# Third layer's input projections: rows turned by token halves, other PSUM banks, pool products moved into the attention

## The chip, the cores and the metric

The kernel is one program on one core of one Trainium2 chip. The metric is the device time in microseconds. Three runs of the kernel before took 1465.88, 1466.32 and 1468.25 us, median 1466.32. Engines: TensorE (PE in the profile, its weight loads PEld), VectorE (DVE), ScalarE (ACT), GpSimd (POOL) and SyncE (SP), which issues the loads of the weights. Each engine works through its own list of instructions in order, and waits on semaphores that the others raise.

## The reference, cut to what matters

256 tokens of width 1024 pass two transformer layers and then a third one, whose start is the place of this case. `ctx` is a second set of 256 tokens, `mod` a vector worked out from a condition, which shifts and scales the normalized rows.

```python
hx = modulate(rmsnorm(x, norm1_g[l]), sh1, sc1)          # the 256 tokens
hc = modulate(rmsnorm(ctx, norm1_g[l]), sh1c, sc1c)      # the 256 context tokens
qx, kx, vx, px = split_projection(hx @ w_in[l])          # 512, 128, 128 and 512 columns
qx = apply_axial_rope(qx, rope)
kx = apply_axial_rope(kx, rope)
kc, vc = split_kv(hc @ w_in[l][:, ATTN_WIDTH:ATTN_WIDTH + 2 * KV_WIDTH])
attn_x = latent_window_attention(qx, kx, vx, kc, vc, attn_sink[l])   # 8 heads, keys of x and of ctx
pool_x = multiscale_pool(px, pool_w[l], pool_scale[l])   # 4 groups: window mean minus token, then 128x128, then scale
x = x + g1 * (jnp.concatenate([attn_x, pool_x], axis=-1) @ w_out[l])
# then: rmsnorm, modulate, a router and 64 experts of which each token takes 8, and a last rmsnorm
```

All is float32.

## The kernel before

Tokens lie in two tiles of 128 rows (token halves 0 and 1). For a product TensorE needs the features on the partitions, so normalized rows are turned by TensorE: 8 transposes a half (`turn_rows`, recorded at L628) write two PSUM banks, and then ACT takes the first four tiles of the half and DVE the other four, multiplying by the scale and adding the shift on the way (`take_turn_mod`, L1350 and L1673). `xT` holds the columns of the tokens, `cT` those of the context. For the turn named `rms1`, half 0 goes through banks 4 and 5 and half 1 through 6 and 7.

Weights stream through a ring of 8 slots of 1 MB; SP issues the load of a slot once TensorE has raised `chunks_used` for what was in it. The third layer's input weights `in_2` are five chunks: keys and values (1), queries (2), pooled columns (2).

The stretch on TensorE runs so. After the last product of the second layer's MLP (L833) it waits for DVE's last addition (`mlp_added`), makes two broadcast rows of the modulation (`mod_row`, L756; banks 2 and 3, then 0 and 1; ACT copies each into `gaterow`), then the context's keys (bank 2, L1051) and values (bank 3, L1055), then turns both halves of x (`rows_ready` comes from DVE, which normalizes half 0 and then half 1), waits for all columns, and makes the keys and values of x. The query panel (L656, banks 0 and 1) follows, the rotation of the keys for the rope (L670, bank 4), then a wait for the finished rope (`roped`), as the pooled panel (L661) writes bank 4 again. The rotation of the queries (banks 6 and 7) follows that panel, then the pool products (L1081: the pooled columns times a matrix that holds the window means; ACT copies the result, `dT`), a small product for the second modulation (L749, bank 0), and the products with the pool weights (L1089, banks 6 and 7), which ACT scales into `xT` (L1592). Only then does the attention start.

The attention (`attention`) goes through 16 units (8 heads for each half of the tokens; numbers 80 to 95 of the program). Each turn of its loop handles several units at once: at even i the scores of units i and i+1 (L701), the turn of the probabilities of unit i-3 (L720), the product with the values of unit i-4 (L732). DVE masks the scores and takes the row maximum (L1806), ACT takes the exponential (L1372), DVE copies the turned probabilities out of PSUM (L1816). Scores of these units lie in banks 0, 1, 6 and 7, turned probabilities in 2 and 3, the results of the first eight units in one of banks 4 and 5 and those of the other eight in the other. `attention` takes `pieces`, other work of TensorE to be placed into given turns of the loop; without any it runs `keep_warm`, two matmuls of 512 columns whose result is not read (L620), after each of the first two pairs of scores. ACT and DVE have `hooks` in their own loops for the same purpose.

The order is written out by hand, engine by engine; no scheduler moves anything. TensorE's third layer stands from L1042 on, ACT's from L1565, DVE's from L2090.

## Time and profile before

| | |
|---|---|
| median of three runs | 1466.32 us |
| the profiled execution | 1468.9 us |
| its span, first to last instruction | 1467.2 us |
| TensorE busy | 1426.4 us (97%) |
| DVE busy | 457.5 us (31%) |
| ACT busy | 210.9 us (14%) |
| POOL busy | 67.5 us (5%) |
| DMA, mean over the span | 251 GB/s |
| mean granted TensorE clock | 0.993 |

The span is that of one execution under the profiler; the profiled execution's own time is 1.7 us longer. A busy share of 97% for TensorE says that it rarely waits, not that it works at its peak. Float32 matmuls appear as two records each, transposes as one, so counts in the timeline are counts of records. Rows of a timeline give start, duration and what was done; a bracket at the end gives the idle time before and who ended it. In the rows of the chain of waits, the durations are cut so that they add up to the span. In the rows by window, the busy time of each engine is followed by the granted clock (1.00 is 2.4 GHz, 0.50 is 1.2 GHz), the DMA engines' busy share and their GB/s.

### The profile page before, as it was taken

Reading aid. Unit: us, or ns where it says so; the run is one execution under the profiler, and the core shown is the slowest. Engines: PE = TensorE matmul, PEld = TensorE weight load, DVE = VectorE, ACT = ScalarE, POOL = GpSimd, SP = SyncE. Lnnn points to the kernel's source line nnn. Section 1 sums busy time; section 2 is a strip of 40 time slices with the busy share of each in tenths; the row PEclk is TensorE's granted clock in tenths of the full one; section 3 lists DMA queues with packets and bytes.
Section 4 is the critical chain, followed back from the end, with each engine's and each line's share of the span. In section 5 each row is a group of like instructions: output and inputs, shape, how many; then the busy total and the mean of one; then the engine's idle time right before and its main releaser. Section 6 shows DMA issues by size and latency. Waiting matters only on the chain.

```text
span 1467.2 us, 17841 instructions
## 1 busy us (share of the span) xinstructions
PE 1426.4 (97%) x6990; PEld 887.1 (60%) x6990; DVE 457.5 (31%) x1035; ACT 210.9 (14%) x515; POOL 67.5 (5%) x101
## 2 busy tenths in 40 slices
PE   8999999999999999999999999999999999999985
PEld 7676585675658867577575675744454445444542
DVE  1136442422542355242245063422111111111113
ACT  2135200000002331000012141200000000000001
POOL 1016200000000010000000000000000000000000
PEclk9999999999999999999999999999999999999997
DMA  9721174464264335664634405589999999998993
GB/s 394 293 82 59 58 275 184 143 245 184 86 229 145 115 116 213 248 254 183 243 148 158 152 21 207 206 346 378 421 421 404 422 421 421 418 421 331 422 421 157
DMA packets 51833, 368.45 MB, mean 251 GB/s; under 512 B 5856, under 2 KB 6064, under 8 KB 7984
## 3 DMA queue, kind: packets, MB, share of 16 engines
q1 hardware_dynamic: 46080, 333.57, 57.0%
q0 software_dynamic: 5392, 32.05, 6.0%
q10 hardware_dynamic: 288, 1.80, 0.3%
q8 instruction: 52, 0.85, 0.2%
q14 instruction: 21, 0.17, 0.0%
HBM read 366.32 MB, written 1.05 MB: 250 GB/s over the span
## 4 chain that ended last, share of the span: by engine, by line
PE 86%; DVE 3%; DMA 1%; issue 0%; ACT 0%; SPq 0%; DVEq 0%
PE ps L833 15%; PE ps L815 13%; PE ps L1222 13%; PE ps L1172 7%; PE ps L1246 6%; PE ps L1204 6%; PE ps L771 6%; PE ps L656 5%; PE ps L732 2%; PE ps L661 2%; PE ps L701 2%; DMA vec_rows<-in_stream 1%; PE ps L794 1%; PE ps L1015 1%; PE ps L1122 1%; PE ps L628 1%
## 5 line engine op out<-in xcount | busy, mean ns | idle before, releaser
L833 PE MATMUL ps<-ring,qk_tiles 128*128 128x512 f32 x512 | 221.4, 592 | 0.0
L815 PE MATMUL ps<-xT,ring 128*128 128x256 f32 x896 | 194.7, 379 | 0.0
L815 PEld LDWEIGHTS ps<-xT,ring 128*128 128x128 f32 x896 | 170.1, 190 | 25.6 <-issue 2.9
L833 PEld LDWEIGHTS ps<-ring,qk_tiles 128*128 128x128 f32 x512 | 97.1, 190 | 118.1 <-issue 117.7
L1222 PE MATMUL ps<-ring,masked_and_probs 128*32 128x512 f32 (+2 forms) x488 | 150.9, 603 | 0.4 <-DMA par<-in_stream 0.4
L1172 PEld LDWEIGHTS ps<-masked_and_probs,mix_rows 128*128 128x128 f32 x896 | 102.5, 192 | 20.8 <-issue 20.8
L656 PE MATMUL ps<-xT,ring 128*128 128x256 f32 x496 | 110.6, 385 | 0.8 <-DVE xT L1666 0.8
L1172 PE MATMUL ps<-masked_and_probs,mix_rows 128*128 128x128 f32 x896 | 107.0, 278 | 0.0
L656 PEld LDWEIGHTS ps<-xT,ring 128*128 128x128 f32 x496 | 95.4, 193 | 14.5 <-issue 1.2
L1204 PE MATMUL ps<-masked_and_probs,probT 128*128 128x512 f32 x216 | 97.2, 593 | 1.0 <-DVE masked_and_probs L2213 1.0
L1246 PE MATMUL ps<-ring,probT 128*32 128x512 f32 (+2 forms) x264 | 83.7, 597 | 1.6 <-DVE probT L2208 1.6
L771 PE MATMUL ps<-ring,xT 128*128 128x512 f32 x192 | 84.0, 593 | 0.0
L1355 ACT ACTIVATE masked_and_probs<-ps 128x512 f32<-128x512 f32 (+1 forms) x62 | 36.5, 593 | 319.4 <-PE ps L1246 185.2
L1222 PEld LDWEIGHTS ps<-ring,masked_and_probs 128*32 128x32 f32 (+2 forms) x488 | 44.3, 128 | 55.6 <-issue 55.5
L1222 PE MATMUL ps<-qk_tiles,masked_and_probs 128*32 128x512 f32 (+2 forms) x248 | 74.6, 594 | 0.0
L1522 ACT ACTIVATE qk_tiles<-ps 128x512 f32<-128x512 f32 x32 | 17.4, 594 | 358.0 <-PE ps L815 343.0
L2213 DVE COPY masked_and_probs<-ps 128x512 f32<-128x512 f32 x27 | 18.7, 691 | 159.4 <-PE ps L1246 159.4
L2202 DVE TENSOR_TENSOR masked_and_probs<-masked_and_probs,ps 128x256 f32<-128x256 f32 x27 | 11.4, 421 | 175.7 <-ACT masked_and_probs L1630 175.7
L1928 DVE TENSOR_TENSOR qk_tiles<-qk_tiles 128x1024 f32<-128x1024 f32 x16 | 19.6, 1225 | 148.2 <-ACT qk_tiles L1522 148.2
L1204 PEld LDWEIGHTS ps<-masked_and_probs,probT 128*128 128x128 f32 x216 | 38.9, 190 | 40.6 <-issue 38.7
L771 PEld LDWEIGHTS ps<-ring,xT 128*128 128x128 f32 x192 | 35.8, 190 | 41.6 <-issue 41.6
L1939 DVE TENSOR_TENSOR y_rows<-ps,y_rows 128x512 f32<-128x512 f32 x32 | 22.1, 691 | 122.2 <-PE ps L833 120.8
(387 smaller groups left out, 1699.8 us busy)
## 6 DMA issues: line engine op xcount, KB each, us to landing
ring<-in_stream SPq DMA_DIRECT2D x205, 1024.0 KB, 7.2
qk_tiles<-in_stream SPq DMA_DIRECT2D x48, 1024.0 KB, 14.4
vec_rows<-in_stream SPq DMA_DIRECT2D x13, 1024.0 KB, 14.5
con<-in_stream SPq DMA_DIRECT2D x13, 1024.0 KB, 14.5
qk_tiles<-in_ada POOLq DMA_DIRECT2D x12, 1024.0 KB, 6.0
y_rows<-in_stream SPq DMA_DIRECT2D x12, 1024.0 KB, 13.4
par<-in_stream SPq DMA_DIRECT2D x12, 1024.0 KB, 15.8
xT<-in_stream SPq DMA_DIRECT2D x12, 1024.0 KB, 16.6
```

The lines of the kernel that those rows point to most:

```text
L656: mm = pe.matmul(ps[0:n, bank, off:off + T], w[:, kk, col:col + n], src[:, k, :], start=bank not in started, stop=k == KT - 1, skip_group_ ...
L661: mm = pe.matmul(ps[:, bank, off:off + n], src[:, k, t * P:(t + 1) * P], w[:, kk, col:col + n], start=bank not in started, stop=k == KT - ...
L701: mm = pe.matmul(scores(i + n)[:, col:col + key.shape[1]], lhs, key, start=True, stop=True)
L732: mm = pe.matmul(ps[:, 4 + g % 2, col:col + w], probT[0:n, u % 2, t * P:(t + 1) * P], val, start=t == 0, stop=t == len(vals) - 1)
L771: mm = pe.matmul(ps[:, q, :], xT[:, k, t * P:(t + 1) * P], ws[k // 2][:, k % 2, half * 512:(half + 1) * 512], start=k == 0, stop=k == KT - 1)
L815: mm = pe.matmul(ps[:, bank, (m % 2) * T:(m % 2 + 1) * T], w[:, kk, m * P:(m + 1) * P], xT[:, k, :], start=bank not in started, stop=k == ...
L833: mm = pe.matmul(ps[:, q, :], hT[:, k, t * P:(t + 1) * P], ws[k // 2][:, k % 2, half * 512:(half + 1) * 512], start=k == 0, stop=k == 7)
L1172: mm = pe.matmul(ps[:, bank + k // 4, (k % 4) * P:(k % 4 + 1) * P], h2[:, t, k * P:(k + 1) * P], select[:, buf, t, :], start=t == 0, stop= ...
L1204: mm = pe.matmul(ps[:, 2 * t + half, :], probT[:, buf, 256 + t * P:256 + (t + 1) * P], yslot[:, half * 512:(half + 1) * 512], start=False, ...
L1222: mm = pe.matmul(ps[cols, 4, :], hg[:, k, cols], ws[a][:, kk, :], start=k == 0, stop=k == KT - 1, skip_group_check=True)
L1246: mm = pe.matmul(ps[a * width:(a + 1) * width, 5 + half, :], probT[:, buf, k * P + a * width:k * P + (a + 1) * width], ws[a][:, k, half * ...
L1355: return act.activation(dst, src, ACT.Copy, **kw)
```

## The change

Five edits, all in the third layer's start:

- The two modulation rows go to banks 6, 7 and 4, 5; they wait for the context's columns in place of DVE's addition, whose wait now stands before the context's keys.
- x's rows are turned by halves: half 0 between the two halves of the context's values, half 1 behind them; the keys and values of x are made for half 0 and then for half 1, each after its own columns.
- The rotation of the keys goes to bank 2 and the small modulation product to bank 3, directly behind it; the pooled panel no longer waits for `roped`.
- The rotation of the queries stands between the two chunks of the pooled panel.
- The pool products and the two pairs of pool-weight products become pieces of the attention's loop (turns 0, 3 and 7), and ACT's copy and its scaling become hooks in its loop (1, 4 and 8). The weights' products go through bank 4, a pair at a time. With pieces given, `keep_warm` is not run here.

On TensorE, the start of the third layer. `con` holds the identity, `qk_tiles` the context's columns, `y_rows` the rows of x, `ring` the weights. Before:

```order
L756 MATMUL ps<-masked_and_probs,con 128x512 [waits mlp_added,modulation_products]
L756 MATMUL ps<-masked_and_probs,con 128x512 x3
L1051 MATMUL ps<-qk_tiles,ring 128x256 [waits slot_full3,modulation_sbuf,xT_by_dve,xT_by_act]
L1051 MATMUL ps<-qk_tiles,ring 128x256 x7
L1055 MATMUL ps<-ring,qk_tiles 128x128 x16
L628 MATMUL ps<-con,y_rows 128x128 [waits rows_ready]
L628 MATMUL ps<-con,y_rows 128x128 x7
L628 MATMUL ps<-con,y_rows 128x128 [waits rows_ready]
L628 MATMUL ps<-con,y_rows 128x128 x7
L1051 MATMUL ps<-xT,ring 128x256 [waits xT_by_dve,xT_by_act]
L1051 MATMUL ps<-xT,ring 128x256 x7
L1055 MATMUL ps<-ring,xT 128x128 x16
```

Now:

```order
L1057 MATMUL ps<-ring,qk_tiles 128x128 x8
L628 MATMUL ps<-con,y_rows 128x128 [waits rows_ready,modulation_sbuf]
L628 MATMUL ps<-con,y_rows 128x128 x7
L1057 MATMUL ps<-ring,qk_tiles 128x128 x8
L628 MATMUL ps<-con,y_rows 128x128 [waits rows_ready]
L628 MATMUL ps<-con,y_rows 128x128 x7
L1063 MATMUL ps<-xT,ring 128x128 [waits xT_by_dve,xT_by_act]
L1063 MATMUL ps<-xT,ring 128x128 x7
L1065 MATMUL ps<-ring,xT 128x128 x8
L1063 MATMUL ps<-xT,ring 128x128 [waits xT_by_dve,xT_by_act]
L1063 MATMUL ps<-xT,ring 128x128 x7
L1065 MATMUL ps<-ring,xT 128x128 x8
```

The eight transposes of half 0 now stand before the context's second eight values, and eight key products of 256 columns have become two groups of eight of 128.

On TensorE, the pooled panel and the start of the attention. `par` holds the pool weights (and serves `keep_warm`), `v_rows` the panel's copy. Before, from the pooled panel's end:

```order
L670 MATMUL ps<-masked_and_probs,con 128x512 [waits proj_sbuf]
L670 MATMUL ps<-masked_and_probs,con 128x512
L1081 MATMUL ps<-y_rows,v_rows 128x256 [waits poolmat_loaded,proj_sbuf]
L1081 MATMUL ps<-y_rows,v_rows 128x256 x7
L749 MATMUL ps<-group_factors,fold_quarters 32x16 [waits modulation_blocks_summed,fold_ready]
L749 MATMUL ps<-group_factors,fold_quarters 32x16 x3
L1089 MATMUL ps<-qk_tiles,par 128x256 [waits roped,pool_sbuf]
L1089 MATMUL ps<-qk_tiles,par 128x256 x3
L701 MATMUL ps<-qk_tiles 128x256 [waits masked_ready,modulation_sbuf,pool_sbuf]
L701 MATMUL ps<-qk_tiles 128x256 x3
L620 MATMUL ps<-par,con 128x512 x2
L701 MATMUL ps<-qk_tiles 128x256 [waits masked_ready]
```

Now:

```order
L661 MATMUL ps<-ring,xT 128x512 x7
L701 MATMUL ps<-qk_tiles 128x256 [waits masked_ready,modulation_sbuf,roped]
L701 MATMUL ps<-qk_tiles 128x256 x3
L1093 MATMUL ps<-y_rows,v_rows 128x256 [waits poolmat_loaded,proj_sbuf]
L1093 MATMUL ps<-y_rows,v_rows 128x256 x7
L701 MATMUL ps<-qk_tiles 128x256 [waits masked_ready]
L701 MATMUL ps<-qk_tiles 128x256 x3
L720 MATMUL ps<-con,masked_and_probs 128x128 [waits probT_sbuf,exp_ready]
L720 MATMUL ps<-con,masked_and_probs 128x128 x3
L1101 MATMUL ps<-qk_tiles,par 128x256 [waits pool_sbuf]
L1101 MATMUL ps<-qk_tiles,par 128x256
L701 MATMUL ps<-qk_tiles 128x256 [waits masked_ready]
```

The first scores now follow the panel directly, the pool products stand where the first `keep_warm` stood, and the four pool-weight products have become two and two.

On ACT, the attention's start as it stands now. `gate_rows` and the like are behind it; `pool_psum` is raised by TensorE's pool products:

```order
L1368 ACTIVATE v_rows<-ps 128x512 [waits chunks_used]
L1368 ACTIVATE v_rows<-ps 128x512
L1385 ACT_TABLE_LOAD [waits probT_psum]
L1385 ACTIVATE masked_and_probs,esum<-masked_and_probs,negmax 128x512 [waits masked_ready]
L1385 ACTIVATE masked_and_probs,esum<-masked_and_probs,negmax 128x512 [waits probT_psum,masked_ready]
L1368 ACTIVATE qk_tiles<-ps 128x512 [waits pool_psum]
L1368 ACTIVATE qk_tiles<-ps 128x512
L1385 ACTIVATE masked_and_probs,esum<-masked_and_probs,negmax 128x512 [waits probT_psum,masked_ready] x3
L1609 ACTIVATE xT<-ps,par 128x256 [waits pool_psum]
L1609 ACTIVATE xT<-ps,par 128x256
```

Before, the copies into `qk_tiles`, the one into `modT` and the four scalings stood between the copies of `v_rows` and the table load.

The diff:

```diff
--- before.py
+++ after.py
@@ -753,7 +753,7 @@
 
                 for half in range(2):
                     f = vector * D + half * 512
-                    mm = pe.matmul(ps[:, 2 * vector + half, :], C("ones"), mod_sum[:, f:f + 512], start=True, stop=True)
+                    mm = pe.matmul(ps[:, 4 + 2 * vector + half, :], C("ones"), mod_sum[:, f:f + 512], start=True, stop=True)
                 mm.then_inc(s_mps, 1)
 
             def out_projection(n0, name, tiles, before_last):
@@ -1040,59 +1040,72 @@
 
 
             pe.wait_ge(s_mod, 2 * MOD_OPS * MLP_STEPS)
-            pe.wait_ge(s_acc, 2 * MLP_STEPS + EARLY)
+            wait_xT("ctx")
             mod_row(1)
             mod_row(0)
-            wait_xT("ctx")
+            pe.wait_ge(s_acc, 2 * MLP_STEPS + EARLY)
             w = chunk(FIRST["in_2"]).rearrange("p (k n) -> p k n", k=8)
 
-            def keys_values(src, col, start):
+            def context_keys_values():
                 for k in range(KT):
-                    pe.matmul(ps[:, 2, col:col + T], w[:, k, 0:P], src[:, k, :], start=start and k == 0, stop=k == KT - 1,
-                              skip_group_check=True)
+                    pe.matmul(ps[:, 2, T:2 * T], w[:, k, 0:P], cT[:, k, :], start=k == 0, stop=k == KT - 1, skip_group_check=True)
                 for t in range(TT):
+                    if t == 1:
+                        pe.wait_ge(s_msb, 3)
+                        turn_rows(y, "rms1", 0)
                     for k in range(KT):
-                        mm = pe.matmul(ps[:, 3, col + t * P:col + (t + 1) * P], src[:, k, t * P:(t + 1) * P], w[:, k, P:2 * P],
-                                       start=start and k == 0 and t == 0, stop=k == KT - 1, skip_group_check=True)
+                        pe.matmul(ps[:, 3, T + t * P:T + (t + 1) * P], cT[:, k, t * P:(t + 1) * P], w[:, k, P:2 * P],
+                                  start=k == 0 and t == 0, stop=k == KT - 1, skip_group_check=True)
+
+            def keys_values(t):
+                cols = slice(t * P, (t + 1) * P)
+                for k in range(KT):
+                    pe.matmul(ps[:, 2, cols], w[:, k, 0:P], xT[:, k, cols], start=False, stop=k == KT - 1, skip_group_check=True)
+                for k in range(KT):
+                    mm = pe.matmul(ps[:, 3, cols], xT[:, k, cols], w[:, k, P:2 * P], start=False, stop=k == KT - 1,
+                                   skip_group_check=True)
                 return mm
 
-
-            pe.wait_ge(s_msb, 2)
-            keys_values(cT, T, True)
-            turn(y, "rms1")
-            wait_xT("rms1")
-            keys_values(xT, 0, False).then_inc(s_used, 1)
+            context_keys_values()
+            turn_rows(y, "rms1", 1)
+            wait_columns("rms1", 0)
+            keys_values(0)
+            wait_columns("rms1", 1)
+            keys_values(1).then_inc(s_used, 1)
             n0 = FIRST["in_2"] + 1
 
-            pe.wait_ge(s_msb, 3)
             panel(n0, set(), ws4(0))
             pe.wait_ge(s_projsb, 13)
-            rotate(C("rot2"), raw[:, 1, 0, :], 4, T).then_inc(s_rot, 1)
-
-            pe.wait_ge(s_roped, 5)
-            panel(n0 + 2, set(), [(t, xT, 0, 512, 4 + t, 0) for t in range(TT)])
-            pe.wait_ge(s_projsb, 14)
-            rotate4(C("rot2"), 0)
-
-            pe.wait_ge(s_projsb, 15)
-            pe.wait_ge(s_poolmat, 16)
-            for g in range(4):
-                for t in range(TT):
-                    mm = pe.matmul(ps[:, 4 + g // 2, (g % 2) * T:(g % 2 + 1) * T],
-                                   v[:, t, 512 + g * P:512 + (g + 1) * P], poolmat[:, g, t, :], start=t == 0, stop=t == 1)
-            mm.then_inc(s_dps, 1)
-
-            mod_columns(1, 16, 0)
-            pe.wait_ge(s_dsb, 1)
+            rotate(C("rot2"), raw[:, 1, 0, :], 2, T).then_inc(s_rot, 1)
+            mod_columns(1, 16, 3)
+
+            def rotate_last():
+                pe.wait_ge(s_projsb, 14)
+                rotate4(C("rot2"), 0)
+
+            panel(n0 + 2, set(), [(t, xT, 0, 512, 4 + t, 0) for t in range(TT)], between=rotate_last)
+
+            def pool_products():
+                pe.wait_ge(s_projsb, 15)
+                pe.wait_ge(s_poolmat, 16)
+                for g in range(4):
+                    for t in range(TT):
+                        mm = pe.matmul(ps[:, 4 + g // 2, (g % 2) * T:(g % 2 + 1) * T],
+                                       v[:, t, 512 + g * P:512 + (g + 1) * P], poolmat[:, g, t, :], start=t == 0, stop=t == 1)
+                mm.then_inc(s_dps, 1)
+
+            def pool_weights(pair):
+
+                pe.wait_ge(s_dsb, pair + 1)
+                for g in range(2 * pair, 2 * pair + 2):
+                    mm = pe.matmul(ps[:, 4, (g % 2) * T:(g % 2 + 1) * T], R("poolw")[:, g * P:(g + 1) * P],
+                                   dT[:, g, :], start=True, stop=True)
+                mm.then_inc(s_dps, 1)
+
             pe.wait_ge(s_roped, 6)
-            for g in range(4):
-                mm = pe.matmul(ps[:, 6 + g // 2, (g % 2) * T:(g % 2 + 1) * T], R("poolw")[:, g * P:(g + 1) * P],
-                               dT[:, g, :], start=True, stop=True)
-            mm.then_inc(s_dps, 1)
-            pe.wait_ge(s_dsb, 2)
-
             pe.wait_ge(s_msb, 4)
-            attention("a2")
+            attention("a2", {0: (pool_products,), 3: (lambda: pool_weights(0),), 7: (lambda: pool_weights(1),),
+                             11: (lambda: pe.wait_ge(s_dsb, 3),)})
             out_projection(FIRST["out_2"], "mix2", 4, lambda: turn_rows(y, "rms2", 0))
 
             def router(t, bank):
@@ -1565,7 +1578,7 @@
             stds()
             for i in range(2):
                 act.wait_ge(s_mps, 2 + i)
-                copy(gaterow[:, 1 - i, :], ps[:, 2 * (1 - i):2 * (1 - i) + 2, :].rearrange("p a b -> p (a b)")).then_inc(s_msb, 1)
+                copy(gaterow[:, 1 - i, :], ps[:, 6 - 2 * i:8 - 2 * i, :].rearrange("p a b -> p (a b)")).then_inc(s_msb, 1)
             mean_squares(s_x3, 0)
             take_turn_mod("rms1", xT, amod[:, 0:8], modT[:, 0:8, 0])
             panel_done("in_2", 1)
@@ -1579,20 +1592,26 @@
             i.then_inc(s_projsb, 1)
             panel_done("in_2", 3)
             copy_panel(raw[:, 0], 0).then_inc(s_projsb, 1)
+            act.wait_ge(s_mps, 4)
+            copy(modT[:, 16:32, 0], ps[:, 3, 0:16]).then_inc(s_msb, 1)
             panel_done("in_2", 5)
             for t in range(TT):
                 i = copy(v[:, t, 512:1024], ps[:, 4 + t, :])
             i.then_inc(s_projsb, 1)
-            act.wait_ge(s_dps, 1)
-            copy_panel(dT, 4).then_inc(s_dsb, 1)
-            act.wait_ge(s_mps, 4)
-            copy(modT[:, 16:32, 0], ps[:, 0, 0:16]).then_inc(s_msb, 1)
-            act.wait_ge(s_dps, 2)
-            for g in range(4):
-                i = act.activation(xT[:, 4 + g, :], ps[:, 6 + g // 2, (g % 2) * T:(g % 2 + 1) * T],
-                                   ACT.Identity, scale=R("poolscale")[:, g:g + 1])
-            i.then_inc(s_dsb, 1)
-            exps("a2", turn_first_half("a2", 4))
+
+            def take_pool_products():
+                act.wait_ge(s_dps, 1)
+                copy_panel(dT, 4).then_inc(s_dsb, 1)
+
+            def scale_pool(pair):
+                act.wait_ge(s_dps, pair + 2)
+                for g in range(2 * pair, 2 * pair + 2):
+                    i = act.activation(xT[:, 4 + g, :], ps[:, 4, (g % 2) * T:(g % 2 + 1) * T],
+                                       ACT.Identity, scale=R("poolscale")[:, g:g + 1])
+                i.then_inc(s_dsb, 1)
+
+            exps("a2", {1: take_pool_products, 4: lambda: scale_pool(0), 8: lambda: scale_pool(1),
+                        **turn_first_half("a2", 4)})
             warm()
             take_turn("mix2", xT, 4, 1)
 
@@ -2097,7 +2116,7 @@
             take_turn_mod("rms1", xT, amod[:, 0:8], modT[:, 0:8, 0])
             sum_blocks(1, mod_sum[:, 2 * D:4 * D])
             dve.wait_ge(s_rot, 5)
-            link(rope(qk[:, 4:5, :], raw[:, 1], 4, C("cos2"), C("sin2"), 1))
+            link(rope(qk[:, 4:5, :], raw[:, 1], 2, C("cos2"), C("sin2"), 1))
             for g in range(2):
                 for o in range(2):
                     i = dve.tensor_copy(qk[o * HD:(o + 1) * HD, 5 + g, :], qk[g * HD:(g + 1) * HD, 4, :])
```

## Rows read from the trace of the kernel before

**Rows 1.** Waits from 785 to 940 us: who waited for whom; total, times, longest

```profile
PE ps L661 <- DVE qk_tiles L2103: 2.5, 1, 2.5
...
PE ps L1051 <- DVE xT L1673: 2.0, 1, 2.0
...
PE ps L701 <- ACT xT L1592: 1.7, 1, 1.7
...
PE ps L1089 <- ACT qk_tiles L1355: 1.0, 1, 1.0
...
PE ps L756 <- DVE y_rows L1939: 0.9, 1, 0.9
```

**Rows 2.** Timeline of TensorE: start, us, what [idle before <- releaser]

```profile
787.07 3.67 PE L756 MATMUL ps<-masked_and_probs,con 128*128 128x512 f32 x8 [0.88 <-DVE y_rows L1939]
...
794.03 3.73 PE L1055 MATMUL ps<-ring,qk_tiles 128*128 128x128 f32 x32
797.60 1.91 PE L628 MATMUL ps<-con,y_rows 128*128 128x128 f32 x16
801.46 5.38 PE L1051 MATMUL ps<-xT,ring 128*128 128x256 f32 x16 [1.95 <-DVE xT L1673]
...
810.25 13.98 PE L656 MATMUL ps<-xT,ring 128*128 128x256 f32 x64
```

**Rows 3.** Chain of waits that ended last: start, us, what

```profile
790.74 3.45 PE ps L1051 x16
...
842.92 3.47 PE ps L1081 x16
...
852.33 1.91 PE ps L620 x4
...
861.43 1.06 PE ps L701 x8
...
865.21 1.06 PE ps L701 x8
...
916.58 3.63 PE ps L1122 x32
```

**Rows 4.** Busy time by window: PE, PEld, DVE, ACT, POOL, clock, DMA, GB/s

```profile
803.00:804.00 1.00, 1.00 (x4) 0.82 (x3) 0.97 (x2) 0.00 (x0) 0.00 (x0) 0.50 1.06 451
...
827.00:828.00 1.00, 0.80 (x2) 0.49 (x3) 0.14 (x1) 0.00 (x0) 0.00 (x0) 1.00 1.00 426
...
857.00:886.00 29.00, 28.89 (x246) 25.76 (x245) 19.68 (x44) 11.13 (x28) 0.00 (x0) 1.00 0.01 2
```

**Rows 5.** Timeline of DVE

```profile
766.97 2.62 DVE L1673 TENSOR_SCALAR qk_tiles<-ps,amod,modT 128x128 f32<-128x128 f32 x8
...
794.26 0.75 DVE L1865 TENSOR_SCALAR y_rows<-x_rows,small 128x1024 f32<-128x1024 f32 x1
...
846.34 0.69 DVE L1687 TENSOR_TENSOR qk_tiles<-qk_tiles,probT 128x512 f32<-128x512 f32 x1
```

**Rows 6.** Timeline of ACT

```profile
798.24 2.90 ACT L1350 ACTIVATE xT<-ps,modT,amod 128x128 f32<-128x128 f32 x8 [2.80 <-PE ps L628]
...
841.24 1.08 ACT L1355 ACTIVATE v_rows<-ps 128x512 f32<-128x512 f32 x2 [15.88 <-PE ps L661]
...
849.58 1.57 ACT L1592 ACTIVATE xT<-ps,par 128x256 f32<-128x256 f32 x4 [2.01 <-PE ps L1089]
851.16 1.28 ACT L1372 ACT_TABLE_LOAD   x1
853.16 0.72 ACT L1372 ACTIVATE masked_and_probs<-masked_and_probs,negmax 128x512 f32<-128x512 f32 x1 [0.71 <-DVE negmax L1806]
```

**Rows 7.** Busy time by window, behind the changed stretch and late in the experts

```profile
847.00:887.00 40.00, 37.69 (x279) 30.54 (x280) 23.33 (x58) 17.67 (x44) 0.00 (x0) 1.00 0.01 2
...
1346.00:1350.00 4.00, 4.00 (x18) 1.06 (x16) 0.00 (x0) 0.00 (x0) 0.00 (x0) 1.00 0.36 154
```

**Rows 8.** Waits of TensorE from 985 us to the end

```profile
PE ps L1222 <- DMA vec_rows<-in_stream: 6.2, 1, 6.2
```

## The prediction

> **What bounds the kernel now.** I read the page first. TensorE is busy for 97% of the span (the table above), so the time to be won or lost is in TensorE's waits and in work of its own that nothing needs. The change lies between the end of the second layer's MLP (786 us) and the start of the third layer's output projection (886 us). For that stretch I read TensorE's waits: only five of them matter, 2.5, 2.0, 1.7, 1.0 and 0.9 us, together 8.1 us [rows 1]. Then TensorE's timeline, to see what stands on both sides of each wait, the granted clock by window, the ACT and DVE timelines to see how late each releaser would be in another order, and last the end of the program, because a gain made at 800 us counts only if the expert stage hands it on.
>
> The chain of waits runs through TensorE for nearly the whole stretch, so its order is the sum. Two things beside the waits stand out. The sixteen records of x's keys (L1051 on xT) took 5.38 us, while the chain puts 3.45 us on the same sixteen for the context [rows 2, 3]; in the window from 803 to 804 the granted clock is 0.50, the lower level of 1.2 GHz [rows 4]. And two groups of L620, four records each, are matmuls whose result nobody reads: 1.91 us each of the chain [rows 3].
>
> **The change, step by step, on the time axis of before.** The last MLP matmul ends at 786.2.
>
> 1. The products for the gate rows no longer wait for DVE's last addition but for the context's columns, which were written by 769.6 (the DVE row that starts at 766.97 takes 2.62 us) [rows 5]. The wait of 0.9 us goes, 0.88 by the gap in the chain; the wait for the addition, over by 787, now stands before the context keys and is past. Banks 4 to 7, the new home, were emptied by the same work.
>
> 2. Turning by halves. Mod rows 3.67, context keys 3.45 and the first half of the values 1.79 (half of the chain's 3.57; the row has 3.73) bring TensorE to 795.1 [rows 2, 3]. It then turns token half 0. Its rows were ready at 795.0 (L1865 at 794.26, 0.75 us) [rows 5]; as ACT's gate copies come some 0.7 us earlier with the earlier products, I expect 794.4. Turning eight tiles costs 0.89 (the sixteen took 1.91 in the row, pipelined) and ends at 796.0, the second values end at 797.8, half 1 is turned by 798.7 (its rows: 797.2 before, about 796.6 now). Taking one half costs ACT half of its 2.90 us and DVE a little less [rows 6]: half 0 is ready at about 798.0, so the keys start at 798.7 without a wait, and half 1 at about 800.1, needed at 802.3. The wait of 1.95 us goes, with margins of 0.7 us or more.
>
> 3. The price of the halves: sixteen matmuls of 256 columns (3.45 us of chain with both records) become 32 records of 128. The only other group of that shape, weights standing and tokens moving, is L1122: 3.63 us of chain for 32 records [rows 3]; the context's values, 32 records of 128, have 3.57. I take +0.12 us; ends 0 and +0.4.
>
> 4. The clock. TensorE fell to the lower level after 1.9 us of transposes and the 1.95 us wait behind them, and 5.38 - 3.45 = 1.93 us went. With no wait there, I take 1.93 us back. Ends: 0 (it falls anyhow, a little later) and 1.93. The wait of 2.54 us at 824.7 had matmuls before it and no fall behind it: the window 827 to 828 shows 1.00 [rows 4]. The Trainium skill (TensorE: Matmul & The Clock Gate, Part 4, PE-mode transpose) says that transposes do not count as busy for the clock gate. The two places agree with that: by it this fall came from transposes and wait together, and eight transposes between matmuls can't bring one (1452.8). If the skill is wrong there, the fall at 803 was a matter of when the clock is looked at, and could come behind another wait as well (1454.7, rival a).
>
> So the second values end at 805.8 instead of 810.4.
>
> 5. Banks and order behind it. The query panel (13.8 us of chain, 13.98 in the row [rows 2]) ends at 819.6, the key rotation (0.45) now goes to bank 2, and the pooled panel writes banks 4 and 5 without waiting for DVE's rope of the keys: the wait of 2.54 us [rows 1] goes. The four small modulation matmuls (0.26 us) only move. They need DVE's block sums, which end 4.6 us behind its turn, near 805. The query rotation stands between the panel's halves; ACT's copy of its input, 1.08 us from 819.6, is done 6 us earlier than needed. TensorE leaves the panel at 836.05 instead of 842.9 with the rotation inside.
>
> 6. The attention's start. Rope of the queries is six DVE operations of 0.69 us [rows 5] from 829.1, done at 833.3; before, it had to run beside the pool products. First scores: 836.05 to 837.1. The pool products (3.47 us of chain [rows 3]) need ACT's copies of the panel, two copies in 1.08 us [rows 6], to 837.2, a wait of 0.1. Second scores 840.7 to 841.7. In this cover DVE masks and ACT takes the exponentials 80 and 81 (table load 1.28, then 0.72 and a 0.19 read each [rows 6], so about 840.1) and then the pool copies, 840.7 to 841.8. Turn of unit 80: 841.7 to 842.2; first pair of pool weights, 1.0 us, needs 841.8. The waits of 1.0 and 1.7 us [rows 1] are thus gone (0.98 + 1.66 = 2.64), and the pool work is the same number of matmuls as before, so it costs what it cost.
>
> 7. The two L620 groups go: 2 x 1.91 = 3.82 us. They had stood as cover while the first exponentials ran; the pool products take that place. One pair of units costs TensorE 3.78 us in the steady part (861.43 to 865.21 [rows 3]); from 857 to 886 DVE is busy 19.68 of 29 us and ACT 11.13 [rows 4], so ACT's two added scale steps (0.8 us each, 1.57 for both before [rows 6]) fit in what it has left.
>
> The pool work interposed costs nothing new if the ACT queue keeps up. Bounds: no wait at all; or the pool weights find the copy 1.1 us late and a scale step once delays a turn by 0.8: up to 1.9 us. I take 0.1, near the margins of 0.4 us and more found above. On this the skill would differ: ScalarE: Activation LUTs, What ACT_TABLE_LOAD costs, gives 2.66 us for a switch with its drain. The profile shows 1.28 us and 0.71 us of idle behind it that DVE's mask explains. By the page the exponentials end near 841.5, the copy near 842.6, and TensorE would wait some 0.4 us more.
>
> Sum: 0.88 + 1.95 - 0.12 + 1.93 + 2.54 + 2.64 + 3.82 - 0.1 = 13.5 us (a little rounding).
>
> 8. Does it reach the end? Everything later is released by TensorE: the expert loads that come first after the attention wait for its end, with the DMA engines idle before them (0.01 busy from 847 to 887) [rows 7]. Late in the expert stage the DMA engines are full and TensorE waits 6.2 us for a slot [rows 8]. That stretch is the danger. But DMA is at 0.36 from 1346 to 1350 [rows 7]: the backlog had been worked off and the last full stretch starts with TensorE's own releases. So it moves with TensorE, and 13.5 us go through whole.
>
> The profiled execution took 1468.9 us, 1.7 over its span of 1467.2, and becomes 1455.4. It is 2.6 us above the median of 1466.32; the same 13.5 from the median is **1452.8 us**.
>
> **Rivals.**
> (a) The clock falls all the same, at the keys or behind another short wait: 1.93 us is not regained, 1454.7. For it: the lower level at 803 came 1.4 us after work had begun again, so it is no immediate reaction. Against: no wait over 1 us is left here.
> (b) The attention starts starved. Without the dummy matmuls, and with pool copies before the third exponential in ACT's queue, TensorE waits there by up to the 3.82 us it saved: 1453.5 to 1456.6. For it: margins of 0.3 to 0.4 us at the first turn of a probability tile and at the pool weights. Against: every release computed comes in time.
> (c) The expert stage absorbs it: the loads are paced by the DMA engines and the end stays at 1466.3. For it: the full DMA engines late in the program and the 6.2 us wait [rows 8]. Against: the gap at 1346 [rows 7].
> (d) Slower. The dummy matmuls held the clock through the attention; without them short 64-column matmuls and transposes let it fall for the rest of the attention. At half rate the 29 us from 857 to 886 would become up to 58, so 1466.3 - 13.5 + 29 = 1482. It decides once more than 13.5 of those 29 us run at the lower level. For it: over a quarter of a pair's 3.78 us is transposes. Against: the same mix ran at 1.00 all that time, 29 us behind the last dummy [rows 4], and products of 256 columns stand in the dummies' place.
> (e) A transfer or copy I placed as early is late, or the order doesn't take the waits away: half the gain, 1460.
>
> **How the numbers follow.** Forecast 0.68 (own range 1451.3 to 1454.0), (a) 0.10, (b) 0.10, (c) 0.04, (d) 0.04, (e) 0.04. The three runs shown spread over 2.4 us, so the 80% range runs from 1450.6, all steps plus a lucky median, to 1457.5, which takes in (a) and (b). About 0.2%, 2.9 us, is what a measurement of this kernel can tell from no change. Faster by more: 0.68 + 0.10 + 0.10 + 0.04 = 0.92; same, case (c), 0.04; slower, case (d), 0.04.
>
> **What would show it.** TensorE's wait list for the stretch has nothing above 0.5 us; the sixteen-record groups of x's keys take 1.8 us each with the clock at 1.00; the pooled panel starts near 820.3; first scores near 836, output projection near 872.5; no L620 in this attention; the wait for a load near the end is still about 6 us. I am wrong if the projection starts at 872.5 and the end does not move with it (c), or if it starts later: then by a wait at the pool weights or first turns (b), or by a clock row below 1.00 (a, d).

## The result and the profile after

| | before | changed |
|---|---|---|
| median, 4 runs each | 1467.01 us (1465.88 to 1468.25) | 1452.78 us (1452.48 to 1454.23) |
| profiled execution, span | 1467.2 us | 1450.9 us |
| mean granted clock | 0.993 | 0.996 |

The ratio is 0.9894, 95% interval 0.9878 to 0.991: 14.2 us faster, where 13.5 (1452.8) had been forecast. The spans differ by 16.3 us, and 2.65 us of that is not the change: from the first transpose to the first layer's attention, code that both share, the profile of before takes 77.52 us and that of after 74.87. The two rows of the first products show it (before, then after; start, us, what):

```profile
9.39 7.83 PE L656 MATMUL ps<-xT,ring 128*128 128x256 f32 x24 [0.83 <-DVE xT L1666]
```

```profile
9.35 5.42 PE L656 MATMUL ps<-xT,ring 128*128 128x256 f32 x24 [0.83 <-DVE xT L1685]
```

The same 24 records took 2.41 us longer in before's execution: 11 of them fall into the window from 9 to 14 us there, 22 in the changed kernel's. The column of the granted clock shows 1.00 in both, so that the clock still stood at the lower level is inferred from this rate. It is luck of the execution and not the change: in a second profile of the changed kernel ("changed again", below) the row took 7.46 us.

So I compare by stages. TensorE's timeline of the changed kernel, start, us, what (all of the changed stretch but the repeating units):

```profile
783.58 3.60 PE L756 MATMUL ps<-masked_and_probs,con 128*128 128x512 f32 x8
...
790.47 1.95 PE L1057 MATMUL ps<-ring,qk_tiles 128*128 128x128 f32 x16
792.25 1.04 PE L628 MATMUL ps<-con,y_rows 128*128 128x128 f32 x8
793.12 1.95 PE L1057 MATMUL ps<-ring,qk_tiles 128*128 128x128 f32 x16
794.91 1.04 PE L628 MATMUL ps<-con,y_rows 128*128 128x128 f32 x8
795.78 1.95 PE L1063 MATMUL ps<-xT,ring 128*128 128x128 f32 x16
...
802.93 13.98 PE L656 MATMUL ps<-xT,ring 128*128 128x256 f32 x64
...
817.46 7.13 PE L661 MATMUL ps<-ring,xT 128*128 128x512 f32 x16
824.43 1.88 PE L670 MATMUL ps<-masked_and_probs,con 128*128 128x512 f32 x4
...
833.11 1.13 PE L701 MATMUL ps<-qk_tiles 64*128 64x256 f32 x8
834.36 3.72 PE L1093 MATMUL ps<-y_rows,v_rows 128*128 128x256 f32 x16
838.01 1.14 PE L701 MATMUL ps<-qk_tiles 64*128 64x256 f32 x8
839.07 0.66 PE L720 MATMUL ps<-con,masked_and_probs 128*128 128x128 f32 x4
839.56 1.03 PE L1101 MATMUL ps<-qk_tiles,par 128*128 128x256 f32 x4
...
869.71 10.52 PE L771 MATMUL ps<-ring,xT 128*128 128x512 f32 x24
```

No row has a bracket: from 784 to 870 us, between the gate products and the output projection, TensorE is idle for 0.23 us in all, of which 0.12 stand before the pool products. Where [rows 2] had 5.38 us for the first keys of x behind a wait, there are groups of 1.95 without one. TensorE's list of waits from 785 to 930 us, which was [rows 1], has one entry, in the router behind the stretch (before's profile has the same 0.7 us there), and the late one, which was [rows 8], stands as it did:

```profile
PE ps L1146 <- ACT mix_rows L1368: 0.7, 1, 0.7
```

```profile
PE ps L1235 <- DMA vec_rows<-in_stream: 6.2, 1, 6.2
```

By window (columns as in [rows 4]): the clock is up where it had been 0.50, it is up in the attention without the unread matmuls, and the DMA engines' late gap of [rows 7] has moved along:

```profile
803.00:804.00 1.00, 1.00 (x6) 0.89 (x6) 0.00 (x0) 0.86 (x3) 0.00 (x0) 1.00 0.00 0
...
843.00:872.00 29.00, 28.88 (x231) 24.84 (x231) 18.91 (x45) 12.88 (x33) 0.00 (x0) 1.00 0.01 1
1330.00:1334.00 4.00, 4.00 (x21) 1.15 (x24) 0.00 (x0) 0.00 (x0) 0.00 (x0) 1.00 0.37 158
```

Stages by the starts of TensorE's rows, and the experiments beside them. "Stage" is from the first gate product (L756) to the output projection; "panel" and "scores" are where the query panel and the first scores start in it; "behind" is from the projection to the last matmul of the program. Each of these stages is read from one profile, each median from all runs of a kernel. The experiments ran in three groups, each on a chip of its own, with runs of the kernel before beside them.

| kernel | panel | scores | stage | behind | median of its runs |
|---|---|---|---|---|---|
| before | 23.18 | 64.13 | 98.78 | 570.15 | 1467.01 (4); beside group A 1468.72 (11), B 1468.40 (17), C 1468.59 (17) |
| changed | 19.35 | 49.53 | 86.13 | 570.02 | 1452.78 (4) |
| changed again | 19.35 | 49.53 | 86.13 | 569.97 | 1456.67 (6), C |
| whole turn | 23.17 | 53.35 | 89.95 | 570.59 | 1458.93 (6), A |
| whole turn, filled | 21.54 | 51.72 | 88.32 | 572.23 | 1458.67 (6), B |
| dummies back | 19.35 | 49.53 | 89.42 | 570.07 | 1457.25 (6), A |
| pool work ahead | 19.36 | 59.39 | 91.07 | 570.68 | 1459.41 (6), A |
| key bank | 19.35 | 51.95 | 88.55 | 572.08 | 1458.99 (6), A |
| rotation behind | 19.35 | 53.77 | 91.82 | 570.64 | 1458.94 (5), B |
| before without dummies | 23.18 | 64.13 | 95.81 | 572.30 | 1467.75 (12), B |
| the same, filled | 23.18 | 64.13 | 95.81 | 569.66 | 1465.43 (12), C |
| no start dummies | 19.35 | 49.53 | 86.13 | 570.75 | 1474.17 (5), B |
| early matmuls | 19.36 | 49.54 | 86.13 | 570.23 | 1455.35 (6), C |
| both additions | 19.35 | 49.53 | 86.13 | 570.83 | 1456.68 (6), C |

The stage lost 12.65 us; the stretch from the second layer's output projection to the first gate product went from 254.08 to 253.04 us, which is the first wait. Together 13.7 us. The medians follow the stages only roughly. For the six experiments that change this stage in the changed kernel, stage and first wait put them 8.0 to 11.5 us below before; the medians are 9.3 to 11.5 us below the before of their own group, single ones up to 1.8 us from what their stage says. So the medians confirm the size of the gain, and what one edit is worth rests on the stages. The last section tells of the clock.

### The profile page after: what moved, and what is told of

Read it like the earlier page. It is cut to its first block, busy times and chain, and to the rows that moved or that the text cites. A ratio compares the mean times of both kernels' runs of the same rounds, so it can differ in the third digit from the quotient of the medians.

```text
span 1450.9 us, 17856 instructions
## 1 busy us (share of the span) xinstructions
PE 1417.8 (98%) x6998; PEld 883.0 (61%) x6998; DVE 457.6 (32%) x1035; ACT 210.5 (15%) x515; POOL 67.5 (5%) x101
## 4 chain that ended last, share of the span: by engine, by line
PE 86%; DVE 2%; DMA 1%; issue 0%; ACT 0%; SPq 0%; DVEq 0%
PE ps L833 15%; PE ps L815 13%; PE ps L1235 13%; PE ps L1185 7%; PE ps L1259 6%; PE ps L1217 6%; PE ps L771 6%; PE ps L656 5%; PE ps L732 2%; PE ps L661 2%; PE ps L701 2%; DMA vec_rows<-in_stream 1%; PE ps L794 1%; PE ps L628 1%; PE ps L1015 1%; PE ps L1135 1%
## 6 DMA issues: line engine op xcount, KB each, us to landing
y_rows<-in_stream SPq DMA_DIRECT2D x12, 1024.0 KB, 13.5
```

## The experiments

**Whole turn.** Both halves turned behind the context's values (shortened; the turn of half 0 between those values is taken out too):

```diff
-            turn_rows(y, "rms1", 1)
-            wait_columns("rms1", 0)
+            turn(y, "rms1")
+            wait_xT("rms1")
```

> The changed kernel, but both token halves of x are turned behind the context's values and the keys wait for all columns. My theory (TensorE's order is the sum): the wait before the keys of x is back, 2.0 us, and the clock falls to 1.2 GHz behind transposes and wait, 1.9 us more: 1456.7 us, with keys of the first half at about twice their 1.8 us. Rival 1 (the halves save nothing, other engines end it anyway): 1452.8. Rival 2 (the clock's fall before was chance, not tied to this place): the wait alone, 1454.9, clock 1.00.

The stage grew by 3.82 us, all before the panel. The keys of the first half, behind a wait of 1.96 us, took 3.46 us for 1.95:

```profile
800.84 3.46 PE L1060 MATMUL ps<-xT,ring 128*128 128x128 f32 x16 [1.96 <-DVE xT L1690]
```

```profile
802.00:804.00 2.00, 2.00 (x11) 2.00 (x11) 1.97 (x2) 0.00 (x0) 0.00 (x0) 0.50 0.78 328
```

**Whole turn, filled.** The same with `keep_warm(2, 0)` behind the turn.

> The kernel of e1 (both halves turned together, keys wait for all columns) with two unread matmuls of 512 columns in the wait. Theory (the clock falls for want of matmuls, transposes do not hold it): the wait of 2 us stays but the clock stays at 1.00, 1454.9 us, so 1.9 us less than e1. Rival (the fall has nothing to do with what stands in the gap): as e1, 1456.7.

The stage is 1.63 us shorter than without the fill; the keys take 2.02 us and the clock stays up:

```profile
800.82 2.02 PE L1060 MATMUL ps<-xT,ring 128*128 128x128 f32 x16 [0.24 <-DVE xT L1691]
```

```profile
802.00:804.00 2.00, 2.00 (x20) 2.00 (x19) 1.97 (x2) 0.00 (x0) 0.00 (x0) 1.00 0.77 324
```

So of the 3.82 us, 2.19 stay with the clock up, the wait above all, and 1.63 are the clock. Both profiled executions took 1459.95 us all the same: the second lost its gain behind the stage (572.23 for 570.59), where the clock fell instead. It is one pair of executions; they agree to 0.01 us up to this stage.

**Dummies back.**

```diff
-                        if i < a + 4 and not pieces:
-                            keep_warm(START_WARM, 4 + (UNITS[a][6] + 1) % 2)
+                        if i < a + 4 and (name == "a2" or not pieces):
+                            keep_warm(START_WARM, 2 if name == "a2" else 4 + (UNITS[a][6] + 1) % 2)
```

> The changed kernel with the two pairs of unread matmuls put back behind the first two pairs of scores (into bank 2). Theory (they cost their full length once the pool products are the cover): +3.82 us less the 0.1 us wait that they hide, 1456.5 us. Rival (they only fill time in which TensorE would wait): no change, 1452.8. Rival on the clock (they held it up): no change of the clock either way, 1.00 in both, would speak against it.

The stage grew by 3.29 us, less than the 3.7 expected. The first pair and the row behind it, 1.82 us from start to next start, as for the second pair:

```profile
834.07 1.98 PE L620 MATMUL ps<-par,con 128*128 128x512 f32 x4
835.89 3.62 PE L1093 MATMUL ps<-y_rows,v_rows 128*128 128x256 f32 x16
```

Two times 1.82 are 3.64 us. They hide the 0.12 us wait before the pool products, and the rows next to them are shorter by some 0.2 us together (pool products 3.54 us from start to next start, 3.65 without the pairs). The clock of the stage is at 1.00 either way. So they are nearly pure cost here.

**Pool work ahead** (shortened). Products, copy, weights (banks 6 and 7) and scaling before the attention, which gets no pieces and no unread matmuls:

```diff
-            attention("a2", {0: (pool_products,), 3: (lambda: pool_weights(0),), 7: (lambda: pool_weights(1),), ...
+            pool_products()
+            pe.wait_ge(s_roped, 6)
+            pool_weights()
+            pe.wait_ge(s_dsb, 2)
+            attention("a2", {99: ()})
```

> The changed kernel with the pool products, their copy, the pool weights and the scaling ahead of the attention again, without the unread matmuls. Theory: waits of 1.1 us before the products, 1.0 before the weights and 1.7 before the first scores, and the attention's start, left without cover, waits about 1.3 us for the first exponential; TensorE reaches the output projection 4.5 to 5 us later, 1457.5 us. Rival (the place of the pool work is worth only the waits of before, 2.6 us, the attention starts without a wait): 1455.4.

The stage grew by 4.94 us, and the four waits of TensorE are the ones expected, in other sizes by up to half a microsecond (total, times, longest):

```profile
PE ps L701 <- ACT xT L1611: 1.7, 1, 1.7
PE ps L1101 <- ACT qk_tiles L1370: 1.3, 1, 1.3
PE ps L1093 <- ACT v_rows L1370: 1.2, 1, 1.2
PE ps L720 <- ACT masked_and_probs L1387: 0.8, 1, 0.8
```

**Key bank.** The rotated keys in bank 4 again, and `pe.wait_ge(s_roped, 5)` before the pooled panel.

> The changed kernel with the rotated keys in bank 4 again, so the pooled panel waits for the rope of the keys. Theory: +2.4 us (the wait of 2.5 us less the 0.2 us of small modulation matmuls that now stand in it), 1455.1 us; the clock stays at 1.00 behind this wait, since the panel before it is matmuls. Rival (any wait of 2 us or more brings the clock down): about 1.9 us more, 1457.0. Rival (the bank change saves nothing): 1452.8.

The stage grew by 2.42 us, and the clock stayed up behind the wait:

```profile
822.87 7.13 PE L661 MATMUL ps<-ring,xT 128*128 128x512 f32 x16 [2.35 <-DVE qk_tiles L2123]
```

```profile
823.00:824.00 1.00, 1.00 (x3) 0.52 (x4) 0.00 (x0) 0.00 (x0) 0.00 (x0) 1.00 0.89 377
```

**Rotation behind.** `rotate_last()` after the whole pooled panel.

> The changed kernel with the rotation of the queries behind the whole pooled panel. Theory (the place between the panel's halves hides the rope of the queries, six DVE operations of 0.69 us): the first scores wait for it, 4.2 us, and nothing covers that, as the pool products are a piece behind the scores: 1457.0 us. Rival (the rotation's place is worth nothing, the rope runs beside other work): 1452.8.

The first scores came 4.24 us later, as expected; the stage grew by 5.69. The other 1.45 us are the clock, which fell behind this longer wait and slowed scores and pool products until it was back (0.97 from 841 to 842):

```profile
837.33 1.79 PE L701 MATMUL ps<-qk_tiles 64*128 64x256 f32 x8 [4.17 <-DVE qk_tiles L1707]
839.05 4.70 PE L1094 MATMUL ps<-y_rows,v_rows 128*128 128x256 f32 x16
```

```profile
838.00:841.00 3.00, 3.00 (x11) 1.94 (x8) 1.43 (x4) 1.06 (x3) 0.00 (x0) 0.50 0.00 0
```

**Before without dummies.** The kernel before, `keep_warm` off at the third layer.

> The kernel before without the unread matmuls at the third layer's attention. Theory (they were mostly on the path, but covered the first exponential): 3.1 us of their 3.82 are gained, a wait of 0.7 us for the exponential takes the rest: 1463.8 us from 1467.0; the clock stays at 1.00. Rival (they held the clock): it falls in the attention and the kernel is slower than before. Rival (pure cover): no change, 1467.

The stage is 2.97 us shorter, with the wait in the place expected. But over 12 runs the median is 1467.75 against 1468.4 (17 runs), ratio 0.9999, interval 0.9987 to 1.0011: no gain in device time is shown. Behind the stage this profile is 2.15 us longer than before's, and there, at the ranking of the tokens, the clock is down:

```profile
853.66 0.66 PE L720 MATMUL ps<-con,masked_and_probs 128*128 128x128 f32 x4 [0.83 <-ACT masked_and_probs L1372]
```

```profile
931.00:936.00 5.00, 5.00 (x32) 4.93 (x31) 1.26 (x5) 0.00 (x0) 0.00 (x0) 0.66 0.63 262
```

**The same, filled.** One unread matmul of 512 columns before the ranking, where TensorE waits 0.74 us and then runs small products:

```diff
             turn_back(1)
+            pe.matmul(ps[:, 7, :], ident, shared_ws[1][:, 0, :], start=True, stop=True)
             rank_tokens()
```

> The kernel before without the unread matmuls at the third layer's attention, and with one unread matmul of 512 columns between the turning back of the second half and the ranking of the tokens (where TensorE waits 0.74 us and then runs small products). Theory (the 3 us that the first edit gained in its stage were taken back by the clock, which fell at that place): the stage still shows 95.8 us, no fall at 49 us behind the output projection's start, median 1465.5 us against 1468.4 of before. Rival (the gain was lost elsewhere): median as without the fill, 1467.8. Rival (the fill costs more than the wait hides): stage behind longer by 0.1 to 0.9 us.

1465.43 us against 1468.59, ratio 0.9976, interval 0.9964 to 0.9987: the 3 us are there. The mean clocks of the runs say the same as the two profiles: without the fill 11 of 12 runs had 0.992 or 0.988 (the profiled one 0.992), with it 9 of 12 had 0.993 or 0.994 (the profiled one 0.994). The two versions ran on different chips, each beside its own before. The fill stands in the wait, and the window is at full clock:

```profile
926.23 1.02 PE L1159 MATMUL ps<-ring,con 128*128 128x512 f32 x2
```

```profile
928.00:934.00 6.00, 6.00 (x52) 5.43 (x53) 2.23 (x8) 1.15 (x3) 0.00 (x0) 1.00 0.69 291
```

**No start dummies.** The changed kernel with `START_WARM = 0`, which touches only the second layer's attention.

> The changed kernel without the unread matmuls at the second layer's attention too, the only ones left (3.8 us of TensorE). Theory: there the first exponential is ready 0.7 us before TensorE comes, so 0.7 us are gained and a wait of 2.7 to 3 us takes the rest: 1452.1 us if the clock stays up; with the clock down behind that wait it loses 1 to 3 us, 1454 to 1455. Rival (pure cost as at the third layer): 3.8 us gained, 1449.0.

Slower than before: 1474.17 us, ratio 1.0035 (1.0022 to 1.0048). That attention grew from 34.94 to 53.87 us. TensorE waited 2.76 us at its start, the clock fell, and it was down until 2 us before the attention's end at 551.75 us:

```profile
501.69 0.30 PE L720 MATMUL ps<-con,masked_and_probs 128*128 128x128 f32 x1 [2.76 <-ACT masked_and_probs L1385]
```

```profile
501.00:550.00 49.00, 48.31 (x198) 43.57 (x199) 22.24 (x93) 18.56 (x66) 0.00 (x0) 0.51 0.03 12
549.00:550.00 1.00, 1.00 (x8) 1.00 (x7) 0.15 (x1) 0.98 (x2) 0.00 (x0) 0.67 0.00 0
```

The 1.9 us before that rise were the attention's eight transposes of finished rows (L628, from 547.49). The wait was forecast (2.7 to 3 us), the length of the fall was not: a loss of 1 to 3 us had been expected.

**Changed again.**

> The changed kernel once more, beside the others on one chip. The first four runs gave 14.2 us, the stages of the two profiles 13.7 (12.65 from the first modulation product to the output projection and 1.0 before it). If the rest is the clock's luck in single executions, the medians on one chip differ by 13 to 15 us and this profile again shows 86.1 us for the stage; if the stage itself scatters, it shows another length.

The stage repeated to 0.01 us, the median did not: 1456.67 us against 1468.59, 11.9 us (ratio 0.9915, 0.9889 to 0.9941). Three of the six runs took 1452.6 to 1454.7 us at a mean clock of 0.995 or 0.996, three 1458.7 to 1461.3 at 0.989.

**Early matmuls**, three of 256 columns before the identity has landed, and **both additions**:

```diff
+            dve.memset(masked[:, 0, 0:384], 0.5).then_inc(s_first, 1)
+            pe.wait_ge(s_first, 1)
+            for _ in range(3):
+                pe.matmul(ps[:, 7, 0:256], masked[:, 0, 0:128], masked[:, 0, 128:384], start=True, stop=True)
```

> The changed kernel with three unread matmuls of 256 columns on a freshly set tile before the identity has landed, in the first 5 us where TensorE is idle. Theory (the clock rises for activity, and the start runs at the lower level until 8 to 14 us after the span's start): the turning of x takes about 1.9 us instead of 3.5 and the first products never run at the lower level; first turn to attention 73 to 74 us instead of 74.9 to 77.5; median 1 to 4 us lower, 1450 us. Rival (three are too few, or the time to the first rise does not depend on them): no change.

> The changed kernel with both additions, the three early matmuls and the one before the ranking. If both work by the clock alone: the median of the run with the early matmuls or up to 2 us lower, and runs closer together, since one of the places at which the clock fell in some executions is closed.

Medians 1455.35 and 1456.68 us, neither told apart from the changed kernel's 1456.67 beside them. The first products did start earlier (8.71 us for 9.35) and at the full rate, which they also had in the changed kernel's first profile; but the turning of x shrank from 3.45 only to 3.00 us:

```profile
1.43 2.93 PE L850 MATMUL ps<-masked_and_probs 128*128 128x256 f32 x6 [1.43 <-DVE masked_and_probs L1982]
4.88 3.00 PE L629 MATMUL ps<-con,x_rows 128*128 128x128 f32 x16 [0.52 <-DMA con<-in_consts]
8.71 5.42 PE L657 MATMUL ps<-xT,ring 128*128 128x256 f32 x24 [0.83 <-DVE xT L1689]
```

In this profile the clock fell once more in the first layer's attention, and the way from its start to the second layer's attention took 421.51 us in place of 415.66 without a fall. The expectation was missed; no version here is shown to beat the changed kernel.

## Why the prediction was right, step by step

1. The first wait: 0.88 forecast, 1.04 found.
2. to 4. Halves and clock: -1.95 + 0.12 - 1.93 = -3.76 forecast for the way to the query panel, -3.83 found (23.18 to 19.35). The whole turn shows that the halves, and not the earlier gate products, are the cause, the fill that the clock's share goes by what stands in the wait. Its size was a little off: 1.6 us in that experiment, 1.93 in the forecast. The price of the halves was 0.12 in the forecast; the rows give 0.13 (keys and values of x, 795.78 to 802.93, are 7.15 us; the context's in before's chain were 3.45 and 3.57).
5. Banks: 2.54 forecast for the wait of before; putting it back cost 2.42. The rotation between the panel's halves, which I priced at nothing, hides more than any other step: behind the panel it costs 5.69, a wait of 4.2 and 1.45 of clock. It is no gain over before, where the rope ran beside the pool products, and so no term of the sum is missing; but the scores can follow the panel only because of it.
6. The pool waits, 2.64 forecast. With all of the pool work ahead, four waits of 5.0 us stand where one of some 0.1 stood, and the stage grows by 4.94.
7. The unread matmuls: 3.82 forecast, 3.29 when put back. As a term of the change it was nearly right: in before's timeline the two pairs take 1.91 and 1.82 us from start to next start, 3.73 together. Put back into the new order they cost less, for the reasons given there. In before's order they were worth 2.97, as they hid 0.83 of the exponential. The Trainium skill (ScalarE: Activation LUTs, What ACT_TABLE_LOAD costs) gives 2.66 us for a switch with its drain. This case's trace does not agree: in the changed kernel the load took 1.28 us and the first exponential started 1.30 us after the load's start.
8. The end: 570.15 against 570.02 us behind the projection. The expert stage moved as a whole.

Rival (a) did not come: the clock is at 1.00 from 784 to 870 us, with no wait above 0.12 us there. Rival (b) didn't happen; (c) neither. Rival (d) didn't happen at the third layer, where the clock is 1.00 without unread matmuls in the changed kernel and in before's order. But as a mechanism it is real: at the second layer's attention taking out the unread matmuls cost 18.9 us net. There nothing else stood in their place and TensorE waited 2.76 us; here the pool products follow the first scores after 0.12 us. I had given (d) 0.04 because the steady mix ran at 1.00 in before. That is weak evidence: the last section has the clock falling inside such a mix in the first layer's attention. In the third layer's, no profile shows a fall except behind the 4.17 us wait; what makes the difference was not tested.

Rival (e) did not happen: every wait named is gone, and the stage, forecast to lose 12.6 us, lost 12.65.

The stages give 13.7 us and the medians 14.2, on a median of before that came out at 1467.01 for the 1466.32 from which I had subtracted. The agreement with 1452.8 to a hundredth is better than the method, and luck: all ten runs of the changed kernel have a median of 1453.6, the six later ones fall in two groups by their mean clock, and beside their own before they are 11.9 us faster, not 14.2.

## What to carry to other kernels

Where one engine carries the chain, write its order with every release time beside it and sum the gaps: steps 2 to 7, summed in that way, gave 12.6 us for the stage and 12.65 came. Fill a cover with work that must be done anyway, and look which wait it covers before dummy work is removed: the same two dummies were worth 3.3 us of loss in one attention and 18.9 us of protection in another. Compare stages of two profiles, not medians of a few runs, when the gain is near what the clock takes and gives: 2.15 us in one stage, up to 5.85 in another.

## What the runs showed of the hardware

- The clock's fall depends on the execution, not only on the kernel. At the ranking of the tokens it fell in three profiles (key bank, whole turn filled, before without dummies: 572.1 to 572.3 us behind) and not in the others (569.7 to 570.8), with the same instructions there but for the fill. In the first layer's attention it fell in five of the fourteen profiles (whole turn, whole turn filled, key bank, early matmuls, both additions; 0.53 to 0.96 in windows of 10 us between 120 and 160 us), though its code is the same in all. So the gain of one edit can be taken back 80 us later: 2.97 us gained and 2.15 lost, and no such loss in the profile with a fill of one matmul.
- A fall needs no wait. In the profile of the whole turn, filled, TensorE was busy for 5.00 of 5 us with short scores, transposes and products of 30 to 128 columns, its longest wait from 114 to 128 us was 0.2 us, and the clock fell all the same:

```profile
120.00:125.00 5.00, 5.00 (x44) 4.31 (x42) 3.10 (x16) 2.36 (x9) 4.69 (x7) 1.00 0.02 3
125.00:126.00 1.00, 0.86 (x6) 0.59 (x4) 0.97 (x8) 0.60 (x3) 0.92 (x2) 0.61 0.00 0
```

- A busy TensorE did not bring it back at once. In the second layer's attention without unread matmuls it was busy for 48.31 of 49 us at a mean clock of 0.51. In the third layer, after the fall at 838 us, the clock was back at 841, with scores and pool products between. Which property of the work decides was not tested.
- Waits of 2.35 and 2.54 us behind a panel of matmuls brought no fall, waits of 1.95 and 1.96 behind transposes did, and so did one of 2.76 behind scores and one of 4.17 behind matmuls. With two unread matmuls in the wait behind the transposes there was none. At the program's start nothing but transposes runs before the first products, for 3.67 us in before's profile and 3.45 in the changed kernel's, where sixteen transposes at 1.00 take 1.91 [rows 2]; the products behind them took 7.83 us in the first and 5.42 in the second, which is the full rate (the next 24 records took 5.35 in both). So in the changed kernel's profile the clock rose with transposes alone behind it, and in the second layer's attention it rose at the end of 1.9 us of them. The Trainium skill (TensorE: Matmul & The Clock Gate, Part 4, PE-mode transpose) says that a transpose does not count as busy for the clock gate in the way that a matmul does. The two falls behind transposes agree with that, the changed kernel's start does not; no run here settles it.
